# A two-layer encoder trunk on one core: part of a gate projection moved in between index scores, a weight exchange spread over two attention steps, and a new order of projection tiles in both layers

## What is computed

```python
# layer 0
a_u, a_v, b_q, b_k, b_v, i_q, i_k, i_w = jnp.split(rms_norm(h, g[0]) @ w_in, splits, axis=-1)
a_out = gelu(a_u) * (w_s masked @ layer_norm(gelu(a_v)) + b_s)         # 8 groups of 128 channels
score = sum over 8 heads of i_w * relu(i_q @ i_k.T)                     # per block of 128 queries
sel = top_k(score, 256)                                                # admissible keys only
b_out = softmax(b_q @ b_k[sel].T / 8 + rel_bias) @ b_v[sel]             # 16 heads, one key head
mix = concatenate([a_out, b_out]) @ w_out
# layer 1
q, k, v = jnp.split(rms_norm(h, g[0]) @ c_w_in, ...)                   # 16 heads, 2 key heads
mix = softmax over a band of two chunks of 64 keys, with a sink, @ v, @ c_w_out
```

## Time and profile before

| what | value |
|---|---|
| runs, median | 2513.18 us |
| profiled execution, its own time | 2521.1 us |
| span of its trace | 2518.9 us |
| mean granted clock of TensorE | 0.985 |
| PE busy | 2410.1 us (96%) |
| DVE busy | 1704.6 us (68%) |
| POOL busy | 1466.0 us (58%) |
| ACT busy | 1182.7 us (47%) |
| share of PE in the chain that ended last | 66% |

### The profile page before, as it was taken

One profiled execution on the slowest core, in us unless ns is written; L12 is line 12 of the kernel. 1 busy time (PEld: TensorE's weight loads), 2 busy tenths in 40 slices (PEclk: granted clock), 3 DMA queues, 4 the chain that ended last, 5 costly groups with the idle time before them and its releaser, 6 DMA issues.

```text
span 2518.9 us, 34099 instructions
## 1 busy us (share of the span) xinstructions
PE 2410.1 (96%) x11680; PEld 1986.5 (79%) x11680; DVE 1704.6 (68%) x2859; ACT 1182.7 (47%) x2025; POOL 1466.0 (58%) x813
## 2 busy tenths in 40 slices
PE   7899999998999999999999999989999999999997
PEld 5689888776777878888778887878777888778886
DVE  5469998676776596555666577167787565666676
ACT  5442633565664374444333336255666444433331
POOL 2111578555554139887678642456636888577951
PEclk9999999999999999999999999989999999999999
DMA  5390544833545624554644444657563545754343
GB/s 147 67 133 26 126 105 140 249 101 91 164 128 184 222 68 142 162 158 146 242 167 153 149 130 138 167 131 180 143 187 104 160 137 165 248 184 147 105 142 133
DMA packets 330515, 369.63 MB, mean 147 GB/s; under 512 B 14002, under 2 KB 229586, under 8 KB 328324
## 3 DMA queue, kind: packets, MB, share of 16 engines
q1 hardware_dynamic: 321748, 351.96, 47.9%
q10 hardware_dynamic: 8352, 15.21, 2.1%
q0 software_dynamic: 272, 0.62, 0.1%
HBM read 237.18 MB, written 130.55 MB: 146 GB/s over the span
## 4 chain that ended last, share of the span: by engine, by line
PE 66%; DVE 6%; ACT 4%; issue 3%; DMA 1%; POOL 1%; SPq 0%; DVEq 0%; ACTq 0%; POOLq 0%
PE ps L470 62%; PE ps L2764 2%; PE ps L2843 1%; DMA h_operand_raw<-h_operand_scratch 1%; ACT junk L1390 1%; DVE acc L1960 1%; ACT logits L1707 1%; PE ps L2773 1%; DVE acc L1979 1%; DVE logits L2276 1%; DVE probs_T L2311 1%; ACT probs_T L1732 1%; DVE xn_T L2063 1%; PE ps L2853 1%; ACT xn_T L1426 0%
## 5 line engine op out<-in xcount | busy, mean ns | idle before, releaser
L470 PE MATMUL ps<-xn_T,w_split 128*128 128x512 f32 (+1 forms) x2928 | 677.8, 390 | 3.6 <-ACT x_sums L1434 2.9
L470 PEld LDWEIGHTS ps<-xn_T,w_split 128*128 128x128 f32 (+1 forms) x2928 | 547.1, 187 | 121.9 <-DVE xn_T L2063 2.6
L470 PE MATMUL ps<-w_operand,h_operand 128*128 128x512 f32 x2016 | 462.5, 391 | 14.3 <-DVE acc L2545 7.5
L470 PEld LDWEIGHTS ps<-w_operand,h_operand 128*128 128x128 f32 x2016 | 380.0, 189 | 96.9 <-issue 13.3
L425 POOL TENSOR_TENSOR w_split<-w_raw,w_split 128x1024 fp32r<-128x1024 f32 x74 | 185.4, 2516 | 455.4 <-ACT w_split L418 455.0
L1304 POOL TENSOR_TENSOR w_split<-w_raw,w_split 128x512 fp32r<-128x512 f32 x168 | 244.3, 1467 | 102.2 <-ACT w_split L1824 100.8
L470 PE MATMUL ps<-x_sums_high,w_split 128*128 128x512 f32 x896 | 284.9, 389 | 0.0
L1336 POOL TENSOR_TENSOR w_operand<-w_block,w_operand 128x2048 fp32r<-128x2048 f32 x42 | 208.5, 4965 | 110.2 <-ACT w_operand L1844 110.2
L2547 DVE TENSOR_TENSOR acc<-acc,ps 128x512 f32<-128x512 f32 x288 | 185.5, 680 | 127.1 <-PE ps L470 126.6
L1831 ACT ACTIVATE h_operand<-h_operand_raw 128x2048 fp32r<-128x2048 f32 (+1 forms) x56 | 95.3, 1701 | 265.3 <-DMA h_operand_raw<-h_operand_scratch 265.3
L2477 DVE TENSOR_TENSOR h_operand<-h_operand_raw,h_operand 128x2048 fp32r<-128x2048 f32 (+1 forms) x56 | 168.0, 3000 | 56.9 <-ACT h_operand L1831 56.6
(11 more groups left out here) (284 smaller groups left out, 4257.1 us busy)
## 6 DMA issues: line engine op xcount, KB each, us to landing
h_operand_raw<-h_operand_scratch SPq DMA_DIRECT2D x42, 1024.0 KB, 5.3
w_raw<-in_w SPq DMA_DIRECT2D x72, 512.0 KB, 8.1
w_block<-in_w SPq DMA_DIRECT2D x48, 512.0 KB, 6.0
q_scratch<-q_split SPq DMA_DIRECT2D x128, 128.0 KB, 2.6
cat_scratch<-attn_out_split SPq DMA_DIRECT2D x128, 128.0 KB, 2.6
w_raw<-in_w_in SPq DMA_DIRECT2D x30, 512.0 KB, 5.0
q_tile<-q_scratch ACTq DMA_DIRECT2D x58, 256.0 KB, 2.7
unit_tile<-cat_scratch SPq DMA_DIRECT2D x56, 256.0 KB, 4.2
```

The source lines that it names most:

```text
L470: return nc.tensor.matmul(out_ap, stat, mov, start=start, stop=stop)
```

## The change

1. **Value product between scores.** Six of the 32 groups of the gate value projection (column pair 0, t 0 to 5) are made in halves of 12 matmuls behind scores 9, 13, 17, 20, 23, 26, 29, 32, 35, 38, 41 and 44; ACT takes each finished group (Gelu) behind the Relu of the next score. `gelu_v` gets another layout, in which column pair 0 lies where `k_stage` was, so ACT first waits for `kv_sp`.
2. **First projections.** The index key tile becomes tile 4 and the last index query tile becomes tile 5. The transposes of v and index weights wait for `A_P0 + 10` only; those of `w_s` get a wait for their own bank.
3. **Lines.** `bias_lines` moves to offset 0 (over the gain rows). DVE no longer waits for `line_sp`. The lines are spilled in eight DMAs of four heads, one behind each weight tile load of the value projection; the gain rows are loaded after them.
4. **Normalizer** at bit 16 instead of 18.
5. **Fills of attention 0.** Two fills in (0, 0); none in (1, 5), (1, 6) and (3, 7); the splitting of tiles 4 to 7 goes one step later. ACT waits for `ao_lo` before its load of query tile 5.
6. **Layer 1.** The last two query tiles are made half 1 first: (8, 1), (9, 1), then the transposes of v, then (8, 0), (9, 0). Their spills follow that order.

```diff
+AV_HALF = {n: divmod(k, 2) for k, n in enumerate((9, 13, 17, 20, 23, 26, 29, 32, 35, 38, 41, 44))}
+AV_TAKE = {n + 1: t for n, (t, half) in AV_HALF.items() if half}
...
-            n = 2 if (i, b) == (1, 4) else 0 if (i, b) in ((1, 5), (3, 0), (3, 7)) else 1
+            n = 2 if (i, b) == (0, 0) else 0 if (i, b) in ((1, 5), (1, 6), (3, 7)) else 1
...
-SWAP_HIGH = {(1, 4, "end"): [4], (1, 5, 5): [5], (1, 5, "end"): [6], (1, 6, 5): [7],
+SWAP_HIGH = {(1, 5, 5): [4], (1, 5, "end"): [5], (1, 6, 5): [6], (1, 6, 6): [7],
              (3, 6, 5): [8], (3, 6, 6): [9], (3, 7, "end"): [10, 11]}
-SWAP_LOW = {(1, 5): ([4, 5], [6]), (1, 6): ([7], []), (3, 7): ([8, 9], [10, 11])}
+SWAP_LOW = {(1, 6): ([4, 5], [6]), (1, 7): ([7], []), (3, 7): ([8, 9], [10, 11])}
...
-    lines = at("bias_lines", [48, REL_SPAN], F32, D0 + 86 * K)
+    lines = at("bias_lines", [48, REL_SPAN], F32, 0)
...
     def q1_slot(f):
-        return ((f // 2, f % 2) if f < 4 else (f % 2, f // 2))
+        if f < 4:
+            return f // 2, f % 2
+        order = (*range(4, 12), 13, 15, 12, 14)
+        place = 4 + order.index(f)
+        return place % 2, place // 2
...
         for n in range(T_AV + 4, T_Q + 4):
             load_tile(sp, n, tile_src(n))
+            l, h = 1 - (n - T_AV - 4) // 4, 4 * ((n - T_AV) % 4)
+            r = 32 * l + h
+            sp.dma_start(lined[l, h:h + 4], lines[r:r + 4, :].unsqueeze(1).to_broadcast([4, P, REL_SPAN])).then_inc(line_sp, 16)
+        sp.wait_ge(ws_ok, 1)
+        sp.wait_ge(line_sp, 128)
+        for g in range(4):
+            load_gain(g)
...
             nc.scalar.activation(rl[:, d, 0:w], ps[:, 2 * d:2 * d + 2, :].rearrange("p a n -> p (a n)")[:, 0:w],
                                  ACT.Relu).then_inc(sc_free, 1)
+            if n in AV_TAKE:
+                act.wait_ge(kv_sp, 32)
+                take_value(0, AV_TAKE[n])
...
-        dve.wait_ge(line_sp, 32)
...
-            if bit == 18:
+            if bit == 16:
                 normalizer()
...
             for n in range(4, T_AV):
-            project_tile(pe, n, A_P0 + 2 * n, m0=IKW0 if n == 5 else 0)
-        pe.wait_ge(a_free, A_P0 + 12)
+            project_tile(pe, n, A_P0 + 2 * n, m0=IKW0 if n == 4 else 0)
+        pe.wait_ge(a_free, A_P0 + 10)
...
             last.then_inc(sc_full, 1)
+            if n in AV_HALF:
+                t, half = AV_HALF[n]
+                gate_value(pe, 0, t, 4 * half, 4 * half + 4)
...
         project_first(pe, 2)
-        for n in range(T_P1 + 4, T_O1):
+        for n in range(T_P1 + 4, T_O1 - 2):
             project_tile(pe, n, A_P1 + 2 * (n - T_P1))
-        pe.wait_ge(a_free, A_SM1)
-        for k in range(2):
-            for b in range(4):
-                last = nc.tensor.transpose(ps[:, (A_SM1 + k) % 4, b * P:(b + 1) * P], vT1[:, (4 * k + b) * P:(4 * k + b + 1) * P], ident[:])
-            last.then_inc(a_full, 1)
+        for th in (1, 0):
+            for n in (T_O1 - 2, T_O1 - 1):
+                f = A_P1 + p1_place(n - T_P1, th)
+                pe.wait_ge(w_lo, n + 1)
+                pe.wait_ge(a_free, f - 3)
+                project_half(n, f, th)
+            for k in range(2 if th else 0):
+                f = A_P1 + 18 + k
+                pe.wait_ge(a_free, f - 3)
+                for b in range(4):
+                    last = nc.tensor.transpose(ps[:, f % 4, b * P:(b + 1) * P], vT1[:, (4 * k + b) * P:(4 * k + b + 1) * P], ident[:])
+                last.then_inc(a_full, 1)
         pe.wait_ge(a_free, A_N3)
...
             if len(fills) == 2:
-                return {0: (fills[0], 0, 2), 1: (fills[0], 2, 4), 3: (fills[1], 0, 2), "end": (fills[1], 2, 4)}
+                return {0: (fills[0], 0, 4), "end": (fills[1], 0, 4)}
...
-            if k == 16:
-                return {2: (k, 0, 1), 4: (k, 1, 2), 6: (k, 2, 3), "end": (k, 3, 4)}
```

More of the change, by code:

```diff
@@ L1527, in evac_p0 @@
                 nc.scalar.activation(vT[:, cs], b[HD:P], ACT.Copy).then_inc(a_hi, 1)
-            elif n < 5:
-                nc.scalar.activation(iq2[0:HD, 2 * n - 2, cs], b[0:HD], ACT.Copy)
-                nc.scalar.activation(iq2[HD:P, 2 * n - 1, cs], b[HD:P], ACT.Copy).then_inc(a_hi, 1)
+            elif n != 4:
+                h = 2 * (n - 1 - n // 5)
+                nc.scalar.activation(iq2[0:HD, h, cs], b[0:HD], ACT.Copy)
+                nc.scalar.activation(iq2[HD:P, h + 1, cs], b[HD:P], ACT.Copy).then_inc(a_hi, 1)
             else:
@@ L1554, in act_program, with take_value @@
             nc.scalar.activation(wsT[:, 0, 4 * k:4 * k + 4, :], ps[:, f % 4, :].rearrange("p (g t) -> p g t", g=4), ACT.Copy).then_inc(a_hi, 1)
+        def take_value(cp, t):
+            f = B_AV + 8 * cp + t
+            act.wait_ge(b_full, f + 1)
+            nc.scalar.activation(v_block(cp)[:, t, :], ps[:, 4 + f % 4, 0:256], ACT.Gelu,
+                                 accum_out=gsum[:, t, cp:cp + 1]).then_inc(b_free, 1)
         for n in range(len(SCORES)):
@@ L1569, in act_program @@
             for t in range(NB):
-                f = B_AV + 8 * cp + t
-                act.wait_ge(b_full, f + 1)
-                nc.scalar.activation(gv[:, t, cp * 256:(cp + 1) * 256], ps[:, 4 + f % 4, 0:256], ACT.Gelu,
-                                     accum_out=gsum[:, t, cp:cp + 1]).then_inc(b_free, 1)
+                if cp or t >= len(AV_TAKE):
+                    take_value(cp, t)
             split_hi(act, T_AV + 2 * cp + 1 + LOOK)
@@ L1602, in v_high @@
                 act.wait_ge(b_full, B_SV + 2 * g)
-            nc.scalar.activation(v_ln(g)[:, 0], gv[:, :, g * P:(g + 1) * P], ACT.Copy).then_inc(vl_hi, 1)
+            nc.scalar.activation(v_ln(g)[:, 0], v_group(g), ACT.Copy).then_inc(vl_hi, 1)
         def gate_gelu(g, ths=(0, 1)):
@@ L1676, in act_program @@
             split_hi(act, T_P1 + 4 + k)
-        for k in range(4, 10):
+        for k in range(4, 8):
             if k + LOOK >= 8:
@@ L1689, in act_program @@
             last.then_inc(a_hi, 1)
+        for k in (8, 9):
+            evac_p1(k, 0, A_P1 + p1_place(k, 0))
         split_hi(act, T_O1 + 3)
@@ L1744, in act_attn0 @@
                 exps(g + 1, j)
+            if g == 0:
+                act.wait_ge(ao_lo, GROUPS - 1)
             if g + 5 < HG * NB:
@@ L2339, in dve_attn0 @@
                     near(g + 1, j)
-                if st == 2 and len(fills) == 2:
+                if len(fills) == 2:
                     take_fill(fills[0])
@@ L2687, in pe_program, with gate_value @@
         pe_ffn(pe, LAYERS[1])
+    def gate_value(pe, cp, t, k0, k1):
+        n = T_AV + 2 * cp
+        pe.wait_ge(w_lo, n + 2)
+        s = n % 4
+        f = B_AV + 8 * cp + t
+        if f >= 4 and k0 == 0:
+            pe.wait_ge(b_free, f - 3)
+        o = ps[:, 4 + f % 4, 0:256].rearrange("p (a m) -> p a m", a=2)
+        for kt in range(k0, k1):
+            xh = xt[:, t // 4, 0, kt, (t % 4) * P:(t % 4 + 1) * P]
+            xl = xt[:, t // 4, 1, kt, (t % 4) * P:(t % 4 + 1) * P]
+            wh = whl[:, s:s + 2, 0, kt * P:(kt + 1) * P]
+            wl = whl[:, s:s + 2, 1, kt * P:(kt + 1) * P]
+            mm(o, xh, wh, kt == 0, False)
+            mm(o, xh, wl, False, False)
+            last = mm(o, xl, wh, False, kt == KT - 1)
+        if k1 == KT:
+            last.then_inc(b_full, 1)
     def qk(stat, kk, w, d, first=0):
```

82 lines of the change are left out of this document (40 added, 42 removed).

## The result

The changed kernel takes 2592.31 us (median of 4 runs, 2588.53 to 2597.81) where the kernel before takes 2512.07 beside it (4 runs, 2508.08 to 2513.3): ratio **1.0319, interval 1.0304 to 1.0333**. It is 80 us slower; the forecast was 12 us faster, with a range from 2487 to 2510 and a chance of 0.04 for any loss. The profiled execution has a span of 2591.6 us and a mean granted clock of 0.971, before 2518.9 and 0.985.

A forecast was written before the change was run, and what follows sets the result against it. PE was taken to bound the kernel, with 66% of the chain. Gains of 3.3 + 4.6 + 3.2 + 1.2 = 12.3 us off the 2513.2 median gave 2500.9 us, with an 8 in 10 range of 2487 to 2510.

The forecast's parts named there:

- first projections: Before the scores: transposes run beside the last tile's evacuation, 2.6 us, and the clock gives 0.7; together -3.3 us.
- value product between scores: Scores of layer 0: 17.3 us of matmuls move in, the scores grow by about 12.7; net -4.6 us.
- lines, gain rows, normalizer, layout: Layer 0, scores to gate stage: the selection and loads have time to spare, so these parts cost 0.
- exchange in attention 0: Attention 0: extra fills cost 4.3 us, steps (1, 4) to (1, 7) save 7.5; net -3.2 us.
- layer 1: Start of attention 1: Exp starts 0.5 us earlier, held by query spills; with logits done in advance, -1.2 us.
- A piece lies ahead of the next weight tile on the DMA rings: ... under 9 us for an eighth: Value product loads: an eighth of the spills takes under 9 us, while a column pair lasts 23 us.
- gaps of PE between 160 and 440: Value product to gate stage: PE gaps in this stretch were named as a sign that the prediction is wrong.
- The rival with late line pieces: Gate stage: ACT, POOL or line pieces late, so only the parts behind it count; 2509 us, chance 0.08.
- the bound that was named: First projections: a gain of only 2.0 us if the lines still wait for PE, DVE's copies ending the chain.
- The ring of two buffers: Scores: PE, ACT and DVE share two buffers; each half delays the ring by 0.8 us, twelve times 9.6.
- The stall in (1, 7): Attention 0: PE waits about 5.3 us for POOL's split of tile 6, plus 1.5 for the clock.
- the rival "the exchange gives nothing": Attention 0: nothing gained beyond two extra fills, the stall has only moved a step; 2505 us, chance 0.12.

The follow-up runs named there:

- quarters: The splits ahead, with the six value groups cut into quarters of 6 matmuls behind 24 scores instead of halves behind 12: 2501.73 us, ratio 0.9947.
- lines16: The changed kernel with each of the eight line pieces holding 16 heads for 32 copies instead of four heads for 128: 2516.88 us, ratio 1.0003.
- the splits ahead: lines16 with POOL's splits of tiles 4 to 7 ahead of step (1, 6)'s output and ACT's layer 1 weight splits moved: 2502.12 us, ratio 0.9948.

## Why the prediction was wrong, step by step

| term | forecast | in the traces | by ratios of runs |
|---|---|---|---|
| first projections | -3.3 | -2.9 | not tried alone |
| value product between scores | -4.6 | -5.2 | -6.5 ± 5 |
| lines, gain rows, normalizer, layout | 0 | +79.3 (71.0 of gaps, 8.3 of clock) | +75 to +79 |
| exchange in attention 0 | -3.2 | +1.3 | +2 ± 4 |
| layer 1 | -1.2 | +3.2 | +5.5 ± 4.5 |

**The step that failed: "A piece lies ahead of the next weight tile on the DMA rings: ... under 9 us for an eighth".** It took the price of a piece from the price of the whole spill, as if bytes alone set it. The whole spill had 16 heads outermost and a piece has 4. The trace of before has no such piece, but it held the warning: the spills alone kept the DMA engines at 0.92 over the scores, at only some 98 GB/s, so the price was one of how the copy is cut up and not of bytes. At a quarter of that rate the eighth is 31 us, and with a piece ahead of every tile the value product and the query projection are bound by the DMA queue. (The sign that the prediction itself named, gaps of PE between 160 and 440, came true.) The Trainium skill, page "DMA: Bandwidth & Descriptors", section "Why a DMA increments its semaphore by 16 and not by 1", has the rule: a copy runs on the largest number of engines up to 16 that divides the slowest dimension of both sides. The runs agree with it: 4, 8 and 16 heads give 2, 4 to 5 and 9 tenths, some 26, 51 and 98 GB/s, and up to 4, 8 and 16 packets under way. The prediction did not weigh this rule, and it is the one that spoke against the change. The rival with late line pieces (chance 0.08) was priced as the loss of the gain ahead of them, 2509; it lacked a rate, so it counted 8 us over the forecast where the kernel is 91 over it.

**First projections: right.** The transposes of v follow the projection without a gap and the scores start at 101.39 instead of 104.33. The last wait ahead of them is for DVE's copies of the lines (2.15 us in after), the bound that was named. The clock gave little: 0.96 in the scores where it was 0.95.

**Value product between scores: right in mechanism and size.** The scores grew from 48.1 to 60.9 us, by 12.8 where 12.7 were forecast, with one activation table load. The ring of two buffers can't save up free time, and quarters, which need less of it at once, cut the growth by 5.5: that is the same mechanism from the other side. How the 12.8 divide into the ring's delay (9.6 forecast) and table and Gelus (3.1) was not measured.

**Exchange: the stall right, its neighbours not.** The stall in (1, 7) was forecast as 5.3 and measured 5.15; the two extra fills were 2.7 and 1.6 and measured 3.1 and 1.7. Two sizes were off. Steps without a fill were to save 2.0: (1, 5) and (1, 6) last 12.68 and 14.82 in lines16 and their twins with a fill, (2, 5) and (2, 6), 12.67 and 14.89, so they save nothing. And (1, 7) lasted 20.93, 8.7 over its twin where 6.8 were counted; the granted clock of that step is 0.84 in after. Together this is what the rival "the exchange gives nothing" said (chance 0.12). With the splits ahead the exchange pays after all: (1, 7) is 7.6 shorter, so by the traces +1.3 becomes -6.3.

**Layer 1: the end right, a wait in front missed.** Exp does stand behind the query spills (5.21 in after). That ACT's next weight split needs the buffer of the very tile whose half is put off was missed; it is a wait that the change adds, with an evacuation queued behind it. It cost 3.2 us instead of a gain. Taken away, the part gains 1.3 us (98.0 against 99.3), and 1.2 were forecast: with ACT's queue in order, the reasoning on the end holds in size too.

**What delays a tile.** SP's blocked issue changes together with the shape of the pieces, so no experiment separates the two. The packets in the trace of after do, for one tile in full. Its load is issued at 167.31 and blocks SP until 177.84. Of its 1024 packets 768, three quarters, go at once, from 178 to 181. The last 256 go from 195.8 to 200.8: they are the share of the engines on which the piece ahead still runs. So of 34.6 us some 10 are the issue and some 20 the wait behind the piece on a quarter of the engines. That quarter never rests: between the first line packet (110.3) and the last (335.0) there are only 1.5 us with none under way. A shorter issue alone would therefore hardly have brought the tiles in faster; why the issue blocks stays open.

**Left open.** Attention 0 starts 7.2 us sooner in the trace of lines16 than in that of before (447.46 and 454.61), and the medians of the two are equal. Most of the 7.2 is spent behind: 1.3 for the exchange and 3.2 for layer 1 leave 2.7, which the interval of the runs (0.9989 to 1.0017) just holds. The spans of the two traces differ by more, 6.7 us: PE's wait for DVE that comes and goes (3.13 and 0.5 us) fell to the trace of before, which is 2.7, and some 1.3 us have no place. What brings that wait about stays open. A difference of a few us between two traces is worth something only where it is read stretch by stretch.

## What to carry to other kernels

A DMA that is cut up is a new shape: cut it so that the outermost dimension of both sides stays at 16, and price a piece by its own shape, not as a fraction of the whole. A slow copy on a queue is paid for by whatever stands behind it there, and prefetching hides it up to a threshold: 18.5 us to landing cost nothing here, 34.6 cost 75 to 79. When the order of tiles is changed, look at each engine's queue for the next use of the buffer whose release moved, and at what stands behind it. The same look explains the gaps here: work that runs ahead (the split of a later tile) and can wait for a DMA stood in ACT's queue in front of work that PE needed now.

## What the runs showed of the hardware

In the same window (165 to 200 us) of three kernels that differ in the shape of the line pieces alone, a 512 KB weight tile lands 7.6 us after its issue began between pieces of 16 heads, with the DMA engines at 9 tenths, 18.5 us between pieces of eight heads at 4 to 5 tenths, and 34.6 us between pieces of four heads at 2 tenths. A queue with most of its engines idle delayed its next transfer more than four times longer than a busy one, since the last quarter of the tile waited for the few engines at work.

A copy is not the only thing that grows longer: with four heads the issues themselves blocked SP for 10 to 16 us each, loads and spills alike, with 16 heads at most 5. But pieces are not needed for that. In the kernel before, the first load of gain rows, issued behind the two whole spills, blocked SP for 37.55 us (113.80 to 151.35).

After a pause of PE of 21 to 28 us the granted clock was 0.78 to 0.83 over the next 14 us, and 1.00 behind them where PE went on (the first and the third); the three pauses cost 8.3 us in this way.
